# Two-layer hybrid decoder: second layer's parameters and phase tables moved into the first block's last steps, last mixer's score maxima placed later

## The chip, the cores and the metric

One core of one Trainium2 chip. The time is device microseconds of the one core. Before the change three runs took 1578.61, 1579.19 and 1581.76 us; the median is 1579.19 us.

## The reference, cut to what matters

x is 256 tokens by 1024 channels, float32, and there are two layers. Each layer does

```
h = h + concat(deltanet(p), s5(p), diff_attention(p)) @ w_out     with p = rms_norm(h) @ w_in
h = h + peer(rms_norm(h))
```

- `s5`: a diagonal complex state space with 16 groups of 64 states. From lambda and the step come a_bar = exp(lambda * step) and the input scale (a_bar - 1) / lambda; a scan over the tokens follows, then C, a skip, a gelu and a gated linear unit. The kernel runs the scan as a real scan of magnitudes between two rotations, so each layer needs tables of cos and sin of the phase for 128 tokens.
- `diff_attention`: 4 heads with two causal softmaxes each; the output is (p0 - lambda p1) V, normalised. lambda is made of exp(sum(lq1*lk1)) - exp(sum(lq2*lk2)) + a constant.
- `peer`: 8 heads per token, top 16 of 128 on two key sets, top 16 of their 256 sums, and for each of these 128 experts per token u_tab[e] . x, gelu, softmax gate, and a weighted sum of v_tab[e]. An expert's u and v rows are 4 KB each, and every token has its own.

Last comes a final rms_norm.

## The kernel before, in words

**Blocks and steps.** The tokens are cut into two tiles of 128, so there are four blocks (layer, tile), numbered i = 0 to 3. The experts of a block are fetched by 128 steps on u_tab and 128 on v_tab. In step r, GpSimd starts one indirect DMA (`u_gather`) that brings the u row of one expert for each of the 128 tokens (512 KB), VectorE takes its dot product with x (`dot`, L1834, 1.22 us), and a second indirect DMA (`v_gather`) brings a v row whose weighted sum TensorE makes (`values`, four rows at a time, on the places 1, 5, 9, ... of a block). This text says "dot 92 of block 0" for step 92 of block 0. There are 512 dots and 512 v gathers in all.

**Rings.** u rows have 7 buffers: the gather for dot q waits for dot q-7. v rows have 11 buffers, freed in fours by `values`; in GpSimd's program the v gather that needs the `values` of place R stands about where the u gather that needs dot R stands. GpSimd issues both kinds in one order, u then v, so one that waits holds back all behind it.

**The mixer of the next block runs beside the dots.** While the dots of block b run, every engine also works on the mixer (norm, input projection, deltanet, s5, attention, output projection, query projection, key scores) of block b+1. This order is written by hand: `mix(i)`, `attention(i)` and `scans(i)` are generators that yield a place, and `Stages.advance(limit)` (L155) runs, after each dot (on TensorE and ScalarE at the same places of their own programs), all that has a place up to the dot's number. Where two parts have the same place, `mix` goes first. `place(i, slot)` and `attend(i, slot)` squeeze the places for i = 1; for i = 2 and 3 they are the numbers in the code. A place only sets the order within an engine's program. Between engines there are semaphores alone, so an engine that waits in a mixer's step also holds back its next dot or its next `values`.

**Top-k.** In places 2 to 22 of each 32 dots VectorE also runs `top` for the next 32 experts, and in the last places of a block `top(4i)` from the new scores.

**Parameters.** SyncE fetches the weights in blocks of 512 KB into a ring of 4 buffers (`wring`, L590), each when TensorE has freed its buffer. `params(1)` (L533) brings the second layer's four: `cols` (317 KB), C (256 KB, into `sa[:, 1024:1536]`), `rows` (486 KB) and `keysT` (512 KB). It is issued once block 1's key scores are done (L580, L581). `keysT` can't be overwritten before those scores.

**Tables.** `tables(i)` (L1356) on VectorE takes the steps, lambda and the sines (two Sin on ScalarE, `tables_sin`) and makes the cos and sin tables `phase_c`, `phase_s` by seven doublings with a scratch A, B in `sa`. Most of its instructions have 8 to 512 columns with a drain between them. It comes in 12 pieces, for the second layer at places 2 to 29 of block 1 (`mix(2)`, L1545 to L1551). Its first piece waits for the parameters (L1360). `outputs(2)` (L1458) folds C into `cz` at place 37.

**Attention of mixer 3** (a "wide" one: second tile, two rounds of two heads each). Each round takes scores on TensorE, `att_max_of` (VectorE reads the scores' maxima from PSUM, L1515), `att_exps` (ScalarE), `att_scales`, `att_second` (ScalarE), `att_diff` (L1531), and the turn of the probabilities on TensorE. Round one's maxima are at place 71 and round two's at 74.6. TensorE's and ScalarE's places are scores 69 and 73.2, exponentials 71.2 and 74.8, turns 75.9 and 78.3. Between them lie the six levels of deltanet's inverse, each a product (71, 74, 77, 80), a copy on ScalarE (71.6, 74.6, ...), an update (72, 75, ...) and on VectorE the mask of a later level (71.6, 74.6, 77.6), which waits for the product two levels before it.

Of the kernel before, what the change touches and what calls it, by code (L numbers as in the profile page):

```python
# [150 lines left out]

SCANS = (33.0, 41.5, 50.0, 58.0)
# [22 lines left out]
def _build(nc, ctx, x, w_blocks, cols_d, rows_d, keys_d, u_tab, v_tab, cst_d, fin_d, out):  # L175
# [148 lines left out]
    params_in = signal("params_in", 64, 0)  # L324
# [120 lines left out]

    def flat3(a):
        return a.rearrange("p a b -> p (a b)")
# [84 lines left out]
    def _(sp):  # L532
        def params(layer):  # L533
            sp.dma_start(cols[:, :], cols_d[layer, :, 0:HELD_COLS]).then_inc(params_in.sem, 16)
            sp.dma_start(sa[:, 1024:1536], cols_d[layer, :, HELD_COLS:HELD_COLS + 512]).then_inc(params_in.sem, 16)
            sp.dma_start(rows[:, :], rows_d[layer, :, 0:HELD_ROWS]).then_inc(params_in.sem, 16)
            sp.dma_start(keysT[:, :, :].rearrange("p h n -> p (h n)"), keys_d[layer, :, :]).then_inc(params_in.sem, 16)
# [40 lines left out]
        for i in range(1, NI):  # L578
            if i == TB:
                sp.wait_ge(*sc_done(1, 2))  # L580
                params(1)  # L581
            for c, (name, half) in enumerate(CHUNKS):
# [8 lines left out]
                if (name, half) == ("out3", 1):  # L591
                    sp.wait_ge(*ao_done(i, 1))
                    sp.dma_start(g2_row, rows_d[i // TB, 0:1, HELD_ROWS:NROWS]).then_inc(g2_in.sem, 16)

# [12 lines left out]
    def _(pe):  # L607
# [383 lines left out]
        def mix(i):  # L991
# [14 lines left out]
            if layer > 0:  # L1006
                pe.wait_ge(*params_in(layer, 64))
# [210 lines left out]
        def head_scores(i, half, banks):  # L1218
            pe.wait_ge(*pq_ready(i, half + 1))
            for j in range(4):  # L1220
                for a in range(2):
                    r = slice(64 * a, 64 * a + 64)
                    ins = mm(banks[a][:, j * P:(j + 1) * P], qpT[r, 4 * half + j, :], keysT[r, 4 * half + j, :])
# [110 lines left out]
    def _(dve):  # L1334
# [21 lines left out]
        def tables(i):  # L1356

            layer = i // 2
            if layer > 0:
                dve.wait_ge(*params_in(layer, 64))  # L1360
# [69 lines left out]
            while n < P:  # L1430
# [3 lines left out]
                A = sa[:, 1536:2048].rearrange("p (m t) -> p m t", m=MT)[:, :, 0:n]  # L1434
                B = sa[:, 2048:2560].rearrange("p (m t) -> p m t", m=MT)[:, :, 0:n]
# [18 lines left out]
            if layer > 0:  # L1454
                yield 37
                outputs(layer)
# [85 lines left out]
        def mix(i):  # L1542
            t, layer = i % 2, i // 2
            rs = rounds(i)
            if t == 0:  # L1545
                yield place(i, 2)
                made = tables(i)
                for k in made:
                    if k > 32:
                        break  # L1550
                    yield place(i, k)  # L1551
# [5 lines left out]
            if t == 0:  # L1557
                yield place(i, 37)
                next(made, None)
# [96 lines left out]
        def attention(i):  # L1656
# [33 lines left out]
            yield attend(i, 71 if wide else 69.8 + 2 * later)  # L1690
            att_max_of(i, rs[0], *round_heads(i, rs[0]))
            yield attend(i, 72.4 if wide else 71.4 + later)
# [4 lines left out]
            yield attend(i, 74 if wide else 72.8 + later)  # L1697
            att_diff(i, rs[0], *round_heads(i, rs[0]))
            if wide:
                yield attend(i, 74.6)  # L1700
                att_max_of(i, rs[1], *round_heads(i, rs[1]))
            if t == 1:
                yield attend(i, 76 if wide else 73.8)
                att_scales(i, rs[1], *round_heads(i, rs[1]))
                yield attend(i, 77.4 if wide else 75.2)
                att_diff(i, rs[1], *round_heads(i, rs[1]))
            yield attend(i, 82 if wide else 80)
            dve.wait_ge(*ao_ss(i, 1))
            V.reciprocal(dss, dss).then_inc(dss_ready.sem, 1)
            yield attend(i, 83.5 if wide else 81.9)  # L1710
# [423 lines left out]
    def _(act):  # L2134
# [20 lines left out]
        def tables_exp(i):  # L2155
            act.wait_ge(*params_in(i // 2, 64))
# [49 lines left out]
        def mix(i):  # L2206
            t, layer = i % 2, i // 2
            rs = rounds(i)
            if t == 0:
                yield place(i, 1)  # L2210
                tables_exp(i)
                yield place(i, 5)
                tables_sin(i)
# [11 lines left out]
            if layer > 0:  # L2225
                act.wait_ge(*params_in(layer, 64))
# [193 lines left out]
        def scans(i):  # L2420
# [248 lines left out]
        for n in range(NP):  # L2669
            if n % 4 == 0:  # L2670
                b = n // 4
                stages = Stages(mix(b + 1), attention(b + 1), *([scans(1)] if b == 0 else [])) if b + 1 < NI else Stages(final_first())
# [159 lines left out]
```

## Time and profile before

| | us |
|---|---|
| median of three runs | 1579.19 |
| the profiled execution, its time | 1580.82 |
| its span (first to last instruction) | 1579.0 |
| VectorE busy | 1104.1 |
| GpSimd busy (issuing gathers) | 993.9 |
| TensorE busy | 970.5 |
| ScalarE busy | 299.6 |

The DMA engines moved 626.51 MB at a mean of 397 GB/s; 536.94 MB of it are gathers. The span and the profiled execution's time differ by 1.8 us, which lie around the span. The steps of the four blocks begin (dot 0) at 131.96, 470.08, 844.98 and 1214.43 us.

### The profile page before, as it was taken

What the parts mean: (1) busy time and instruction counts of PE and PEld (TensorE: products, weight loads), DVE (VectorE), ACT (ScalarE), POOL (GpSimd) and SP (SyncE); (2) the same over time, 40 slices, a digit from 0 to 9 for tenths busy, and PEclk for the clock granted to TensorE, in tenths of its full rate; (3) what the DMA queues carried; (4) which work ended last, traced back from release to release, by engine and by line L of the source; (5) the groups of instructions that cost most, each with busy time, mean ns of one, the idle gap of its engine ahead of it and who ended that gap; (6) DMA issues with size and microseconds to landing.
All of it is one profiled execution on the core that took longest, in us unless ns stands there. A gap on an engine that the chain in (4) does not pass through costs nothing.

```text
span 1579.0 us, 17672 instructions
## 1 busy us (share of the span) xinstructions
PE 970.5 (61%) x5842; PEld 546.2 (35%) x5842; DVE 1104.1 (70%) x2869; ACT 299.6 (19%) x837; POOL 993.9 (63%) x1034
## 2 busy tenths in 40 slices
PE   9996567967443279886644347978864333333335
PEld 8885445534300046552420025755340000000001
DVE  6849799884648978786486766888466757575440
ACT  7434221321100042241100032324110010000000
POOL 0006666776566776667567775656767777777773
PEclk9997889977756589998876678989875666666558
DMA  9558999999999999999999999999999999999997
GB/s 368 188 200 302 411 393 419 419 419 420 418 420 419 381 417 420 419 419 414 420 419 420 420 419 419 408 418 348 418 419 420 419 419 419 419 419 419 420 419 307
DMA packets 172467, 626.51 MB, mean 397 GB/s; under 512 B 19284, under 2 KB 19412, under 8 KB 172376
## 3 DMA queue, kind: packets, MB, share of 16 engines
q0 software_dynamic: 147456, 536.94, 84.0%
q1 hardware_dynamic: 24920, 88.45, 14.2%
q8 instruction: 46, 0.75, 0.2%
q14 instruction: 45, 0.37, 0.1%
HBM read 624.26 MB, written 1.05 MB: 396 GB/s over the span
## 4 chain that ended last, share of the span: by engine, by line
DMA 28%; DVE 21%; POOL 21%; PE 16%; issue 9%; DVEq 4%; ACT 1%; POOLq 0%; ACTq 0%
DMA uring<-in_u_tab,small 24%; PE ps L609 16%; DVE uring L1834 10%; POOL uring L2688 7%; POOL vring L2688 7%; POOL gd L2688 2%; DMA vring<-in_v_tab,small 2%; POOL wring L2688 1%; DMA uring<-in_v_tab,small 1%; DMA sa<-in_u_tab,small 1%; POOL sa L2688 1%; DVE small L1749 1%; DVE small L1760 0%; DVE sel L1794 0%; DVE small L1802 0%
## 5 line engine op out<-in xcount | busy, mean ns | idle before, releaser
L1834 DVE CUSTOM_DVE_ANT_0 uring<-uring,ps 128x1024 f32<-128x1024 f32 x462 | 558.2, 1217 | 282.9 <-DMA uring<-in_u_tab,small 262.1
L2688 POOL DMA_INDIRECT uring<-in_u_tab,small x462 | 452.6, 980 | 371.9 <-DVE small L1834 168.4
L609 PE MATMUL ps<-vring,wmat 128*32 128x512 f32 x1748 | 320.1, 853 | 361.9 <-DMA vring<-in_v_tab,small 305.9
L2688 POOL DMA_INDIRECT vring<-in_v_tab,small x437 | 417.6, 956 | 154.6 <-issue 127.5
L609 PEld LDWEIGHTS ps<-vring,wmat 128*32 128x32 f32 x1748 | 58.1, 137 | 551.2 <-DMA vring<-in_v_tab,small 369.5
L609 PE MATMUL ps<-hnT,wring 128*128 128x128 f32 x1184 | 150.5, 285 | 0.7 <-DMA wring<-in_w_blocks 0.7
L609 PEld LDWEIGHTS ps<-hnT,wring 128*128 128x128 f32 x1184 | 141.4, 198 | 25.8 <-issue 21.6
L609 PE MATMUL ps<-wring,hnT 128*128 128x512 f32 (+1 forms) x208 | 88.6, 573 | 15.4 <-DMA wring<-in_w_blocks 11.6
L2678 ACT ACTIVATE small<-small 128x32 f32<-128x32 f32 x16 | 3.7, 230 | 465.7 <-DVEq L1843 465.7
L609 PE MATMUL ps<-gd 128*128 128x128 f32 (+1 forms) x518 | 74.2, 296 | 12.8 <-ACT gd L2138 11.2
L2138 ACT ACTIVATE gd<-ps 128x512 f32<-128x512 f32 (+3 forms) x86 | 48.0, 564 | 176.2 <-PE ps L609 161.9
L609 PEld LDWEIGHTS ps<-gd 128*128 128x128 f32 x518 | 68.2, 204 | 31.2 <-issue 15.4
L1834 DVE CUSTOM_DVE_ANT_0 gd<-gd,ps 128x1024 f32<-128x1024 f32 x40 | 48.8, 1220 | 32.6 <-DMA gd<-in_u_tab,small 31.1
L609 PEld LDWEIGHTS ps<-wring,hnT 128*128 128x128 f32 x208 | 41.1, 208 | 56.3 <-issue 49.9
L609 PE MATMUL ps<-phase_c,wmat 128*32 128x512 f32 x28 | 24.9, 1043 | 42.6 <-DMA vbuf<-in_v_tab,small 42.6
L609 PE MATMUL ps<-kT,wmat 128*32 128x512 f32 x28 | 25.0, 1046 | 41.2 <-DMA vring<-in_v_tab,small 34.0
L609 PE MATMUL ps<-wring,wmat 128*32 128x512 f32 x112 | 23.6, 989 | 39.2 <-DMA wring<-in_v_tab,small 32.2
L2435 ACT ACTIVATE small<-small 128x16 f32<-128x16 f32 x32 | 6.6, 209 | 215.9 <-DVE small L1782 215.8
L609 PE MATMUL ps<-sa,cz 128*32 128x128 f32 x224 | 33.5, 325 | 20.8 <-DVEq L1509 20.8
L2688 POOL DMA_INDIRECT gd<-in_u_tab,small x40 | 38.3, 958 | 12.2 <-issue 9.8
L1834 DVE DVE_READ_ACCUMULATOR2_ANT small<- 128x1 f32 x512 | 42.3, 83 | 0.0
L609 PE MATMUL ps<-cst 128*128 128x512 f32 x70 | 39.8, 656 | 1.7 <-ACTq L2176 1.7
(450 smaller groups left out, 1507.3 us busy)
## 6 DMA issues: line engine op xcount, KB each, us to landing
wring<-in_w_blocks SPq DMA_DIRECT2D x120, 512.0 KB, 7.2
vring<-in_w_blocks SPq DMA_DIRECT2D x32, 512.0 KB, 8.6
uring<-in_u_tab,small POOLq DMA_INDIRECT x462, 12.5
vring<-in_v_tab,small POOLq DMA_INDIRECT x437, 11.3
wring<-in_cols SPq DMA_DIRECT2D x3, 512.0 KB, 6.8
h<-in_x SPq DMA_DIRECT2D x2, 512.0 KB, 9.2
keysT<-in_keys SPq DMA_DIRECT2D x2, 512.0 KB, 13.7
rows<-in_rows SPq DMA_DIRECT2D x2, 486.0 KB, 10.6
```

What stands on the lines that cost most here:

```text
L609: return nc.tensor.matmul(o, a, b, start=start, stop=True, skip_group_check=True)
L1749: V.max_index(si[:, hd, a, 0:8], sv[:, hd, a, 0:8], S[:, hd, a, :])
L1834: V.tensor_tensor_reduce(row_, row_, xp, 1.0, 0.0, ALU.mult, ALU.add, dots[:, j:j + 1]).then_inc(dot_done.sem, 1)
L2138: return S.activation(dst, src, ACT.Copy, scale=scale)
L2435: S.activation(gate[:, hd, :], gate[:, hd, :], ACT.Exp, accum_out=gz[:, hd:hd + 1])
L2678: S.activation(gt, gt, ACT.Tanh, scale=GELU).then_inc(gelu_tanh.sem, 1)
L2688: nc.gpsimd.indirect_dma_start(dst, None, table, bass.IndirectOffsetOnAxis(ap=index, axis=0)).then_inc(done.sem, 16)
```

## The change

1. SyncE: `params(1)` now brings only `cols`, C and `rows`, and is issued in block 0's part of the weight loop, behind the load of the last block of the output projection of mixer 1 (`out3`, first half), after a wait for `mix_ready(1)`. `keysT` is fetched alone where `params(1)` stood, on its own semaphore, for which TensorE waits before the key scores of blocks 2 and 3.
2. VectorE and ScalarE: `tables(2)` leaves `mix(2)` and becomes a part of its own beside mixer 1. Its first piece is at place 92 of block 0, the next at 95, 96 and 97, the doublings at 99 to 105 and 106.5. ScalarE's exponential of the steps is at 91.5 and its sines at 92.5. The scratch is in `gd` instead of `sa`. `outputs(2)` stays at place 37 of block 1.
3. VectorE's attention places: in mixer 3 the first maxima go from 71 to 73, scales 72.4 to 75, difference 74 to 76; second maxima 74.6 to 77.6, scales 76 to 79, difference 77.4 to 81; the two steps of the output's norm 82 to 84 and 83.5 to 85.5. In mixer 2 the maxima go from 71.8 to 71.9 and the scales from 72.4 to 72.6. In mixer 1 the maxima go from 69.8 to 70.9 and the scales from 71.4 to 72.1 (before squeezing).

```diff
+TABLES = 92.0
-    params_in = signal("params_in", 64, 0)
+    params_in = signal("params_in", 48, 0)
+    tables_at = [(sa[:, 1536:2048], sa[:, 2048:2560]), (gd[:, 2048:2560], gd[:, 2560:3072])]
...
             sp.dma_start(rows[:, :], rows_d[layer, :, 0:HELD_ROWS]).then_inc(params_in.sem, 16)
-            sp.dma_start(keysT[:, :, :].rearrange("p h n -> p (h n)"), keys_d[layer, :, :]).then_inc(params_in.sem, 16)
...
             if i == TB:
                 sp.wait_ge(*sc_done(1, 2))
-                params(1)
+                sp.dma_start(keysT[:, :, :].rearrange("p h n -> p (h n)"), keys_d[1, :, :]).then_inc(keys_in.sem, 16)
...
+                if i == 1 and (name, half) == ("out3", 0):
+                    sp.wait_ge(*mix_ready(i, 1))
+                    params(1)
...
         def head_scores(i, half, banks):
             pe.wait_ge(*pq_ready(i, half + 1))
+            if i >= TB:
+                pe.wait_ge(keys_in.sem, 32)
...
-            if layer > 0:
-                yield 37
-                outputs(layer)
+        def next_tables(i):
+            yield TABLES
+            for k in tables(i):
+                yield TABLES + 0.5 * k
...
-            yield attend(i, 71 if wide else 69.8 + 2 * later)
+            yield attend(i, 73 if wide else 70.9 + later)
             att_max_of(i, rs[0], *round_heads(i, rs[0]))
-            yield attend(i, 72.4 if wide else 71.4 + later)
+            yield attend(i, 75 if wide else 72.1 + later / 2)
             att_scales(i, rs[0], *round_heads(i, rs[0]))
...
-                yield attend(i, 74.6)
+                yield attend(i, 77.6)
                 att_max_of(i, rs[1], *round_heads(i, rs[1]))
...
-                stages = Stages(mix(b + 1), attention(b + 1), *([scans(1)] if b == 0 else [])) if b + 1 < NI else Stages(final_first())
+                stages = Stages(mix(b + 1), attention(b + 1), *([scans(1), next_tables(TB)] if b == 0 else [])) if b + 1 < NI else Stages(final_first())
+        def next_tables(i):
+            yield TABLES - 0.5
+            tables_exp(i)
+            yield TABLES + 0.5
+            tables_sin(i)
```

## Rows read from the trace of the kernel before

**Rows 1.** The page: gigabytes per second in 40 slices, and the chain by line.

```profile
GB/s 368 188 200 302 411 393 419 419 419 420 418 420 419 381 417 420 419 419 414 420 419 420 420 419 419 408 418 348 418 419 420 419 419 419 419 419 419 420 419 307
...
DMA uring<-in_u_tab,small 24%; PE ps L609 16%; DVE uring L1834 10%; POOL uring L2688 7%; POOL vring L2688 7%; POOL gd L2688 2%; DMA vring<-in_v_tab,small 2%; POOL wring L2688 1%; DMA uring<-in_v_tab,small 1%; DMA sa<-in_u_tab,small 1%; POOL sa L2688 1%; DVE small L1749 1%; DVE small L1760 0%; DVE sel L1794 0%; DVE small L1802 0%
```

**Rows 2.** Busy time by stretches of 20 us; last columns: TensorE clock, DMA share, GB/s.

```profile
520.00:540.00 20.00, 6.87 (x32) 1.19 (x32) 18.17 (x60) 0.00 (x0) 14.78 (x15) 0.59 0.97 367
540.00:560.00 20.00, 4.60 (x24) 0.95 (x28) 18.80 (x40) 1.25 (x3) 14.74 (x16) 0.50 1.01 396
...
1060.00:1080.00 20.00, 17.53 (x98) 10.80 (x99) 16.22 (x46) 8.51 (x25) 11.18 (x12) 0.91 0.93 344
1080.00:1100.00 20.00, 16.84 (x124) 10.97 (x123) 18.03 (x39) 8.79 (x31) 14.56 (x15) 0.91 0.96 353
```

**Rows 3.** Stretches in blocks 0 and 1: PE, PEld, DVE, ACT, POOL busy, clock, DMA share, GB/s.

```profile
372.00:408.00 36.00, 26.62 (x193) 19.59 (x192) 14.54 (x24) 5.61 (x9) 19.50 (x22) 0.81 1.03 419
...
474.00:552.00 78.00, 25.92 (x124) 4.21 (x116) 70.38 (x254) 3.58 (x9) 54.43 (x56) 0.59 1.01 400
```

**Rows 4.** VectorE in the 12 stretches of the table pieces: first piece, and their sum.

```profile
474.51:477.66 3.15, 2.31 (x20) 0.93 1.03 421
...
sum 28.54, DVE 23.09; mean DVE 1.92
```

**Rows 5.** What VectorE waited for, 340 to 408 us.

```profile
DVE uring L1834 <- DMA uring<-in_u_tab,small: 35.9, 20, 3.8
```

**Rows 6.** Timeline: SyncE's load of output blocks 2 and 3, TensorE's use of blocks 0 and 1.

```profile
355.32 0.81 SPq L590 DMA_DIRECT2D wring<-in_w_blocks  x2
...
361.33 8.80 PE L609 MATMUL ps<-wring,hnT 128*128 128x512 f32 x16 [4.18 <-DMA wring<-in_w_blocks]
```

**Rows 7.** DMA issues between 410 and 420 us: size, us from issue to landing.

```profile
rows<-in_rows SPq DMA_DIRECT2D x1, 486.0 KB, 10.9
cols<-in_cols SPq DMA_DIRECT2D x1, 317.0 KB, 6.4
sa<-in_cols SPq DMA_DIRECT2D x1, 256.0 KB, 8.9
```

**Rows 8.** Timeline, GpSimd: u gathers for dots 100 and 112 of block 0.

```profile
361.72 0.94 POOL L2688 DMA_INDIRECT uring<-in_u_tab,small  x1 [0.31 <-issue]
...
397.69 0.94 POOL L2688 DMA_INDIRECT uring<-in_u_tab,small  x1 [1.25 <-DVE small L1834]
```

**Rows 9.** Timeline, VectorE: dots 92 and 112 of block 0.

```profile
352.82 1.22 DVE L1834 CUSTOM_DVE_ANT_0 uring<-uring,ps 128x1024 f32<-128x1024 f32 x1 [1.29 <-DMA uring<-in_u_tab,small]
...
418.40 1.21 DVE L1834 CUSTOM_DVE_ANT_0 uring<-uring,ps 128x1024 f32<-128x1024 f32 x1
```

**Rows 10.** Gather and dot of step 89 of block 1, then of step 94 of block 2.

```profile
714.90 0.94 POOL L2688 DMA_INDIRECT uring<-in_u_tab,small  x1 [0.30 <-issue]
...
723.34 1.22 DVE L1834 CUSTOM_DVE_ANT_0 uring<-uring,ps 128x1024 f32<-128x1024 f32 x1 [0.20 <-DMA uring<-in_u_tab,small]
...
1105.02 0.93 POOL L2688 DMA_INDIRECT uring<-in_u_tab,small  x1 [0.30 <-DVE small L1834]
...
1111.09 1.22 DVE L1834 CUSTOM_DVE_ANT_0 uring<-uring,ps 128x1024 f32<-128x1024 f32 x1 [1.32 <-DMA uring<-in_u_tab,small]
```

**Rows 11.** What VectorE waited for, 1050 to 1093 us.

```profile
DVE small L1515 <- PE ps L609: 5.0, 2, 3.2
DVE small L1709 <- ACT small L2414: 0.9, 1, 0.9
DVE sa L1531 <- ACTq L2183: 0.8, 1, 0.8
```

**Rows 12.** Timeline: exponentials on ScalarE, values of place 73 on TensorE, the next v gather.

```profile
1059.09 0.47 ACT L2174 ACTIVATE sa<-ps,small 128x256 f32<-128x256 f32 x1 [5.03 <-DVEq L1518]
...
1065.30 1.96 PE L609 MATMUL ps<-vring,wmat 128*32 128x512 f32 x16
...
1067.57 0.97 POOL L2688 DMA_INDIRECT vring<-in_v_tab,small  x1 [3.26 <-PE ps L609]
```

More of the change, by code:

```diff
@@ L1006, in mix @@
             if layer > 0:
-                pe.wait_ge(*params_in(layer, 64))
+                pe.wait_ge(*params_in(layer, 48))
             for k in range(KT):
@@ L1359, in tables @@
             if layer > 0:
-                dve.wait_ge(*params_in(layer, 64))
+                dve.wait_ge(*params_in(layer, 48))
                 lam_sums()
@@ L1433, in tables @@
                 nc_, ns_ = pw[1] if n in (1, 4, 16, 64) else pw[0]
-                A = sa[:, 1536:2048].rearrange("p (m t) -> p m t", m=MT)[:, :, 0:n]
-                B = sa[:, 2048:2560].rearrange("p (m t) -> p m t", m=MT)[:, :, 0:n]
+                A = tables_at[layer][0].rearrange("p (m t) -> p m t", m=MT)[:, :, 0:n]
+                B = tables_at[layer][1].rearrange("p (m t) -> p m t", m=MT)[:, :, 0:n]
                 pcb, psb = bc(pc[:, :, None], [P, MT, n]), bc(psn[:, :, None], [P, MT, n])
@@ L1544, in mix @@
             rs = rounds(i)
[L1545 to L1551, printed above, removed]
             if i >= TB:
@@ L1558, in mix @@
                 yield place(i, 37)
-                next(made, None)
+                outputs(layer)
             yield place(i, 42)
@@ L1696, in attention @@
                 att_max_of(i, rs[1], *round_heads(i, rs[1]))
-            yield attend(i, 74 if wide else 72.8 + later)
+            yield attend(i, 76 if wide else 72.8 + later)
             att_diff(i, rs[0], *round_heads(i, rs[0]))
             if wide:
-                yield attend(i, 74.6)
+                yield attend(i, 77.6)
                 att_max_of(i, rs[1], *round_heads(i, rs[1]))
             if t == 1:
-                yield attend(i, 76 if wide else 73.8)
+                yield attend(i, 79 if wide else 73.8)
                 att_scales(i, rs[1], *round_heads(i, rs[1]))
-                yield attend(i, 77.4 if wide else 75.2)
+                yield attend(i, 81 if wide else 75.2)
                 att_diff(i, rs[1], *round_heads(i, rs[1]))
-            yield attend(i, 82 if wide else 80)
+            yield attend(i, 84 if wide else 80)
             dve.wait_ge(*ao_ss(i, 1))
             V.reciprocal(dss, dss).then_inc(dss_ready.sem, 1)
-            yield attend(i, 83.5 if wide else 81.9)
+            yield attend(i, 85.5 if wide else 81.9)
             dve.wait_ge(*ao_scaled(i, 1))
@@ L2155, in tables_exp @@
         def tables_exp(i):
-            act.wait_ge(*params_in(i // 2, 64))
+            act.wait_ge(*params_in(i // 2, 48))
             S.activation(stp, col("lst"), ACT.Exp).then_inc(step_ready.sem, 1)
@@ L2208, in mix @@
             rs = rounds(i)
[L2209 to L2213, printed above, removed]
             yield place(i, 33.5)
@@ L2225, in mix @@
             if layer > 0:
-                act.wait_ge(*params_in(layer, 64))
+                act.wait_ge(*params_in(layer, 48))
             for b, o in enumerate((M0, M1)):
@@ L2671, in _ @@
                 b = n // 4
-                stages = Stages(mix(b + 1), attention(b + 1), *([scans(1)] if b == 0 else [])) if b + 1 < NI else Stages(final_first())
+                stages = Stages(mix(b + 1), attention(b + 1), *([scans(1), next_tables(TB)] if b == 0 else [])) if b + 1 < NI else Stages(final_first())
             for j in range(PAIR):
```

## The prediction

> **What bounds the kernel now.** I read the page's slices first. From slice 7 on the DMA engines move 418 to 420 GB/s nearly everywhere, and the chain of waits names the u gathers first, then VectorE's dots and GpSimd's issue of gathers [rows 1]. A 512 KB gather at 419 GB/s is 1.25 us, so one dot's pair is 2.5 us. The total of bytes is fixed and the change doesn't alter it. So the time falls only by what it removes of the idle time of the DMA engines, and rises by what it adds. Then I read the stretches of 20 us, to price the dips. 520 to 560 us lacks (419-367)/419*20 + (419-396)/419*20 = 3.6 us; 1060 to 1100 us lacks 3.6 + 3.15 = 6.7 us [rows 2]. The first dip is that of the tables: from 474 to 552 us VectorE is busy 70.4 of 78 us, the rest being drains, and the DMA engines move 400 GB/s, which is again 3.6 us short [rows 3]. The second lies in mixer 3's attention, where VectorE waits 5.0 + 0.9 + 0.8 = 6.7 us for others [rows 11].
>
> **The tables leave block 1.** Twelve pieces take 28.5 us of VectorE [rows 4]. Without them VectorE needs far less than the 80 us that the DMA engines need for these 32 dots, so the dip's 3.6 us come back. They cannot bring more: outside the dip there was no idle time to recover. Bounds 3 to 4 us. Gain 3.6.
>
> **The tables enter block 0.** In the old trace the place looks made for them: from 340 to 408 us VectorE waits 35.9 us for gathers [rows 5]. But the first piece waits for the parameters, on the engine that runs the dots.
> - Issue. SyncE loads output blocks 2 and 3 at 355.3 and is done at 356.1 [rows 6]; `mix_ready` is given by then. The three parameter DMAs follow up to 357.4.
> - Landing. Alone in SyncE's queue they landed 6.4, 8.9 and 10.9 us after their issue [rows 7]; that would be 368.2. Here four weight loads stand in front. TensorE gets the first two at 361.33 [rows 6]. Rows 7 show `rows` (486 KB) landing about 2.5 us behind C, which is half of 419 GB/s; at that rate two more loads end at 366.3 and the 1059 KB behind them (1.5 + 1.2 + 2.4) at 371.4. I take 371.4, since the first pair's wait is a row of this very place.
> - VectorE ends dot 92 at 354.0 [rows 9] and then stands until 371.4. Queued behind the wait are dots 93 and on; for dot 93 waits the u gather 100, and behind that every later gather on GpSimd. With the first piece (3.15 us) VectorE is free at 374.6, dot 93 ends at 375.7, and gather 100 is issued 14 us later than its 361.72 [rows 8]. ScalarE stands too, but has nothing due.
> - After that VectorE is full: up to dot 106 it has 13 dots (14.8 us), 23 us of pieces (28.5 less the first and, by estimate, 2.2 for the last), and by estimate 4 us of gelu, residual and norm (14.5 busy in 372 to 408 less ten dots, and the part before 372 [rows 3]). That is 3.2 us per dot against 2.5: it doesn't catch up here.
> - What the DMA engines notice. At 397.7 the old kernel issues gather 112 [rows 8]; the new one is at gather 106. It lacks 6 pairs (15.0 us) and four query weight loads (5.0 us), which wait for TensorE, hence for the norm of dot 98; it has 2.6 us of parameters more. Shortage 17.4 us. The spare: gather 112 took at most 20.7 us to its dot [rows 8, 9], while in block 1 a gather took 8.4 us and in block 2 one took 6.1 us with the engines still nearly full [rows 10]. So 12.3 to 14.6 us of the queue could be lost free of charge, and 2.8 to 5.1 us of idle time remain. I take 4.0, their middle. With the landing at 368.2 it would be about 0.8; with VectorE 4 us later still, 8. So 1 to 8.
>
> The Trainium skill, DMA: Bandwidth & Descriptors, section on queues, rings and completion order, says that each DMA engine alternates between the queues it has work for, packet by packet. By it the parameters get half of the bandwidth but stay behind SyncE's own four loads, which is the 371.4 and the 4.0; by the landing times of rows 7 alone it would be the 368.2 and the 0.8. The half rate in rows 7 agrees with the rule.
>
> **keysT alone, and its wait on TensorE.** It is issued where it was, most of a block ahead of its use (block 1 starts at 470 us, block 2 at 845): nothing, covered by block 1's mixer. `outputs(2)` stays. The scratch in `gd` costs what that in `sa` does.
>
> **Attention of mixers 1 and 2.** For mixer 2, 71.8 to 71.9 and 72.4 to 72.6 cross no dot and no other step: nothing. For mixer 1 maxima and scales move one dot; the DMA engines are full there, and they can only change the spare by about 1 us either way. Taken as 0.
>
> **Attention of mixer 3.** Placed two dots later, the first maxima no longer wait for TensorE's scores. But VectorE arrives, by its dots and top-k steps, at about 1058.3, after the scores are there; so the maxima end some 0.8 us later than before, not earlier. ScalarE's exponentials hang on them (it waited 5.0 us for them at 1059.09), behind these the copy for level 3, TensorE's update, the `values` of place 73 at 1065.30, and the v gather that GpSimd holds back until 1067.57 [rows 12]. That v gather, not the dot, is the last wait in this place; it gets later by 0.8. The second maxima, at place 77.6, stand behind the mask of level 6 and come out at about 1076.5 against 1073; TensorE's turn and the `values` of place 77 follow some 2.6 us later, and so does the v gather on them. VectorE meanwhile runs some 5 us ahead and then waits for the output's norm. By my walk through the four programs GpSimd is even with the old kernel again at about 1091. So 0. Bounds: all 6.7 us back if TensorE's chain keeps its time, 2 us lost if the chain's delay lasts.
>
> **Sum.** The profiled execution took 1580.8: -3.6 + 4.0 + 0 gives 1581.2. It stands 1.6 us above the median of the runs, so for a median 1579.6 us. A measurement tells about 0.2%, 3.2 us, from no change; this is within it.
>
> **Rivals.**
> 1. *The old idle time is real room* (faster). The parameters land near 368, or the queue's spare is as large as 20 us; then block 0 costs 0 to 1 instead of 4, and in mixer 3 VectorE's freed waits reach GpSimd for about half of 6.7. Time: 1579.2 - 3.6 + 0.5 - 3.3 = 1572.8. For it: 35.9 us of waits against 28.5 us of tables, and that VectorE's waits and the DMA engines' loss in mixer 3 are the same 6.7 us. Against it: the order of waits worked out above.
> 2. *The parameter wait becomes the bound* (slower). Place: VectorE behind dot 92, about 354 to 371 us, and the dots up to 108 that follow without a gap. Price: each microsecond of VectorE's lag above about 12 us is a microsecond of idle DMA; with the landing at 374 or ScalarE's sines late, the lag is 18 to 20 and the price 8, with the mixer's chain 1 more. Time: 1579.2 - 3.6 + 9 = 1584.6. For it: the latencies of rows 8 to 10 leave no more than 15 us. Against it: the dots of this place were waiting anyway.
> 3. *The change does not do what it says*: the tables' dip goes, block 0 gives the same back, and the attention's places only exchange one wait for another. That is the forecast itself.
>
> **How the numbers follow.** Forecast (within 0.2%) 0.42; rival 1, 0.33; rival 2, 0.25. The forecast's own range is 1576 to 1583. To hold 8 in 10 the range takes in most of rival 1 and rival 2: 1571 to 1585. Faster 0.33, same 0.42, slower 0.25.
>
> **What would show it.** Stretches of 20 us from 500 to 560 at 419 GB/s; if not, the first gain is wrong. A VectorE wait of 15 to 18 us at the first table instruction in block 0 and a dip of some 4 us between 385 and 430: absent, rival 1; twice as deep, rival 2. In mixer 3 no wait of L1515 for TensorE, a later wait at L1709 of some 4 us, and a GpSimd wait for TensorE of 6 to 7 us at place 73; a dip of 5 to 8 us in 1060 to 1100 as before. If that dip shrinks to 3 us, my reading of who holds back GpSimd is wrong.

## The result, and the profile after

The changed kernel took 1585.82 us, median of 7 runs (1583.68 to 1589.93), the kernel before 1581.07 us beside it (7 runs, 1578.61 to 1583.1). The ratio is 1.0040, 95% interval 1.0029 to 1.0050: 6.3 us slower by the ratio, 4.75 by the two medians. The profiled execution of after took 1585.07 us (span 1583.3) against the 1580.82 of before, so 4.25 us are to be found between the two traces. The forecast was 1579.6 us and "within 0.2%", with a range up to 1585.0: the median lies 0.8 us above its top, and a real loss stands where none was forecast. In some of the sets of runs below, each with its own runs of the kernel before on the same chip, every kernel took 1690 to 1745 us (one run of the move alone 2110) and scattered by 2%, so that a ratio from them tells little under 0.4%; they are called scattering sets.

First the page of after: gigabytes per second in 40 slices.

```profile
GB/s 371 183 200 307 406 404 419 419 419 392 396 420 420 419 419 420 419 404 410 420 419 420 420 419 419 419 415 324 419 419 420 419 419 419 419 419 420 419 419 299
```

Counted from slice 0, and against [rows 1], the dip of slice 13 (381) has gone, two new ones stand in slices 9 and 10 (392, 396), one in slices 17 and 18 (404, 410), and the old one of slice 27 is deeper (324 for 348). Now the same by stretches of 20 us; last columns TensorE's clock, DMA share, GB/s.

```profile
380.00:400.00 20.00, 9.17 (x44) 4.59 (x48) 17.10 (x76) 3.92 (x6) 10.51 (x12) 0.50 0.93 350
400.00:420.00 20.00, 19.08 (x172) 14.70 (x164) 18.10 (x63) 1.68 (x3) 11.83 (x13) 0.99 1.00 390
...
520.00:540.00 20.00, 7.28 (x32) 1.19 (x32) 11.26 (x23) 0.00 (x0) 15.12 (x17) 0.50 1.02 419
540.00:560.00 20.00, 7.79 (x35) 1.79 (x36) 12.76 (x28) 4.11 (x6) 15.12 (x17) 0.50 1.03 420
...
680.00:700.00 20.00, 15.82 (x90) 10.19 (x94) 18.31 (x49) 7.70 (x26) 9.07 (x10) 0.83 1.01 405
700.00:720.00 20.00, 15.44 (x120) 10.01 (x112) 14.57 (x30) 11.05 (x37) 15.42 (x16) 1.00 1.00 391
...
1060.00:1080.00 20.00, 14.63 (x70) 9.15 (x70) 15.99 (x37) 6.35 (x19) 7.51 (x9) 0.83 0.83 308
1080.00:1100.00 20.00, 16.07 (x124) 10.31 (x124) 14.92 (x35) 10.78 (x30) 13.30 (x14) 1.00 0.93 337
```

Each stretch is turned into idle time of the DMA engines as in the prediction, (419 - GB/s)/419*20. For before, 380 to 420 moved 419 in both stretches and 680 to 740 moved 419, 414 and 414.

| idle DMA, us | 380 to 420 | 500 to 560 | 680 to 740 | 1060 to 1100 |
|---|---|---|---|---|
| before | 0 | 3.8 | 0.5 | 6.7 |
| after | 4.7 | 0 | 2.2 | 9.2 |
| difference | +4.7 | -3.8 | +1.7 | +2.5 |

The differences sum to 5.1; a dip of 1.0 us at 980 to 1000, which before has and after has not, brings that to 4.1, and the two executions differ by 4.25. Both moved the same bytes, so the idle time of the whole span has to differ by just that; the rest (0.8 us less ahead of 380, 0.8 more behind the last gathers) cancels. The new dip in block 0 is nearly paid for by the old one in block 1, and what is left over lies in the attentions of mixers 2 and 3.

How much of such a difference one execution can carry is seen where the programs are the same. Eight of the eleven profiles outside the scattering sets ("undisturbed" below) are of kernels with the same work up to 340 us; their idle time ahead of 380 us is 59.0 to 62.7. At 680 to 740, before and the three kernels that differ from it only in mixer 3 have 0.5, 1.0, 2.1 and 0.4. So the +1.7 there isn't clear of the scatter; the +4.7 and -3.8 are. At 1060 to 1100 the six with both old rounds of mixer 3 have 4.1 to 6.7, the three with both new ones 7.6 to 9.2.

Block 0, timeline of after: SyncE's parameter issues, VectorE's first table instruction, GpSimd's u gather for dot 100.

```profile
353.91 0.43 SPq L537 DMA_DIRECT2D cols<-in_cols  x1
354.38 0.44 SPq L538 DMA_DIRECT2D sa<-in_cols  x1
354.86 0.43 SPq L539 DMA_DIRECT2D rows<-in_rows  x1
...
370.31 0.23 DVE L1352 CUSTOM_DVE_ANT_0 small<-rows 128x64 f32<-128x64 f32 x1 [17.91 <-DMA rows<-in_rows]
...
374.94 0.94 POOL L2690 DMA_INDIRECT uring<-in_u_tab,small  x1 [13.13 <-DVE small L1835]
```

The parameters landed by 370.3 (371.4 forecast) although they were issued some 2 us earlier than forecast, VectorE stood 17.9 us (17.4), and the gather went out at 374.94 (375.7 forecast). The Trainium skill, DMA: Bandwidth & Descriptors, section on queues, rings and completion order, has each engine take packets from its queues in turn; by it the parameters, behind SyncE's own loads, were to be late in this way. The 15.4 us from the issue of `rows` to VectorE's start, against 10.9 in [rows 7], agree.

Mixer 3's attention in block 2, timeline of after: the first maxima on VectorE, the exponentials on ScalarE, the update and `values` on TensorE, the v gather on GpSimd.

```profile
1057.30 1.22 DVE L1835 CUSTOM_DVE_ANT_0 uring<-uring,ps 128x1024 f32<-128x1024 f32 x1 [2.78 <-DMA uring<-in_u_tab,small]
...
1059.68 1.27 DVE L1523 TENSOR_REDUCE small<-ps 128x2 f32<-128x512 f32 x2
...
1061.26 0.47 ACT L2175 ACTIVATE sa<-ps,small 128x256 f32<-128x256 f32 x1 [8.74 <-DVEq L1526]
...
1063.94 3.78 PE L614 MATMUL ps<-gd 128*128 128x128 f32 x16 [6.08 <-ACT gd L2139]
1067.66 2.69 PE L614 MATMUL ps<-vring,wmat 128*32 128x512 f32 x16
...
1070.66 0.94 POOL L2690 DMA_INDIRECT vring<-in_v_tab,small  x1 [10.36 <-PE ps L614]
```

Set against [rows 12]: exponentials 2.2 us later, `values` of place 73 2.4 us later and 0.7 longer, the v gather 3.1 us later. GpSimd, which waited 3.26 us for TensorE, waits 10.36. Some 0.6 us of this is no work of the attention: block 2 itself begins 0.55 us later (845.53 for 844.98), and counted from its first dot the v gather is 2.5 us later (225.1 for 222.6). The maxima now stand behind dot 73, and dot 73 itself had to wait 2.78 us for its gather. TensorE's granted clock, 0.91 of full speed at 1060 to 1080 before, is 0.83 after.

### The profile page after: what moved, and what is told of

Read it like the earlier page. It is cut to its first block, busy times and chain, and to the rows that moved or that the text cites. A ratio compares the mean times of both kernels' runs of the same rounds, so it can differ in the third digit from the quotient of the medians.

```text
span 1583.3 us, 17676 instructions
## 1 busy us (share of the span) xinstructions
PE 968.7 (61%) x5842; PEld 545.1 (34%) x5842; DVE 1105.9 (70%) x2869; ACT 299.8 (19%) x837; POOL 992.0 (63%) x1034
## 4 chain that ended last, share of the span: by engine, by line
DMA 30%; POOL 21%; DVE 19%; PE 16%; issue 9%; DVEq 3%; ACT 1%; ACTq 0%; SPq 0%; POOLq 0%
DMA uring<-in_u_tab,small 21%; PE ps L614 16%; DVE uring L1835 9%; POOL vring L2690 8%; POOL uring L2690 8%; DMA vring<-in_v_tab,small 4%; DMA gd<-in_u_tab,small 3%; POOL gd L2690 2%; DMA rows<-in_rows 1%; DMA uring<-in_v_tab,small 1%; POOL wring L2690 1%; DVE small L1761 0%; DVE sel L1795 0%; DVE small L1803 0%; PE ps L617 0%
## 5 line engine op out<-in xcount | busy, mean ns | idle before, releaser
L614 PE MATMUL ps<-gd 128*128 128x128 f32 (+1 forms) x518 | 74.6, 297 | 16.6 <-ACT gd L2139 15.1
## 6 DMA issues: line engine op xcount, KB each, us to landing
uring<-in_u_tab,small POOLq DMA_INDIRECT x462, 12.6
```

The lines of the kernel that those rows point to most:

```text
L614: return nc.tensor.matmul(o, a, b, start=start, stop=True, skip_group_check=True)
```

## The experiments

All times are against the kernel before, run beside it on the same chip, and the difference in us is (ratio - 1)*1580. What fell on a scattering set was measured again (ending in _b, _c). No kernel but the one before was measured on two undisturbed sets, so how far a ratio itself moves from set to set isn't known. The ledger of idle DMA is worked out as above, from one profiled execution each.

Theories at the outset. **T1**: the loss is made in mixer 3's attention, and the move of the tables is about neutral. **T2**: VectorE's wait for the parameters is what it costs. **T3**: the one place in mixer 2 does.

### The move alone, and the places alone

`move_only` is the changed kernel with this undone; `places_only` is the kernel before with this done:

```
-            yield attend(i, 71 if wide else 69.8 + 2 * later)
+            yield attend(i, 73 if wide else 70.9 + later)
-            yield attend(i, 72.4 if wide else 71.4 + later)
+            yield attend(i, 75 if wide else 72.1 + later / 2)
...
-            yield attend(i, 83.5 if wide else 81.9)
+            yield attend(i, 85.5 if wide else 81.9)
```

> The changed kernel with every attention place of before: only the parameters and the tables move. T1 (the loss is made in mixer 3's attention, by the first maxima that come later and the chain ScalarE's exponentials, TensorE's update, `values`, v gather behind them; the move gives 3.7 us back in block 1 and costs 4.0 to 4.7 in block 0): 0 to +1.5 us against before, so 1579 to 1581 us, with the dip at 380 to 420 us and none at 520 to 560, and a v gather of place 73 that waits 3 us for TensorE as before. T2 (VectorE's 17.9 us for the parameters behind dot 92 are what the change costs, by a lag carried on): +4 to +6 us, as the whole change.

> The kernel before with the attention places of the change, nothing else. T1: +3.5 to +5.5 us (2.6 us of idle DMA in 1060 to 1100, 1.6 in mixer 2's attention at 680 to 720, and what follows from them). T2: within 1 us of before.

In a scattering set: 1.0040 (0.9997 to 1.0083) and 1.0043 (1.0003 to 1.0083), which decides nothing. Again:

> The changed kernel with every attention place of before, a second measurement for the same reason. T1: 0 to +1.5 us against before (4.0 to 4.7 us lost at 380 to 420 us, 3.7 gained at 500 to 560). T2: +4 to +6 us.

> The kernel before with the attention places of all mixers from the change, nothing else; a second measurement, since the first stood on runs that scatter by 2%. T1 (the loss is made in the attention places): +3.5 to +5.5 us against before, with the v gather of place 73 in block 2 some 3 us later after the block's start. T2 (the parameter wait of block 0 costs it): within 1 us of before.

The move alone: 1.0019 (1.0010 to 1.0027), +3.0 us. The places alone: 1.0030 (1.0021 to 1.0039), +4.7 us. T1 is right of the size of all places together and wrong of the move, which isn't neutral; T2 is too large for the move and wrong of the places. T1's sign was smaller than expected: the v gather of place 73 was to come some 3 us later after the block's start and came 1.3 later (223.9 us for 222.6). The stretches of 20 us of the move alone:

```profile
380.00:400.00 20.00, 8.32 (x43) 4.41 (x46) 17.07 (x76) 3.92 (x6) 10.53 (x12) 0.60 0.91 341
400.00:420.00 20.00, 18.80 (x172) 14.72 (x164) 17.92 (x63) 1.69 (x3) 11.83 (x13) 1.00 1.00 388
...
680.00:700.00 20.00, 15.79 (x96) 10.85 (x98) 17.08 (x49) 7.95 (x27) 9.91 (x12) 0.91 1.02 410
700.00:720.00 20.00, 15.71 (x120) 10.08 (x112) 15.98 (x32) 10.83 (x37) 15.42 (x16) 1.00 1.01 398
720.00:740.00 20.00, 13.92 (x56) 4.74 (x56) 12.79 (x27) 1.34 (x5) 15.12 (x17) 0.83 1.02 408
```

5.2 us idle in block 0, none at 520 to 560, and 2.0 us at 680 to 740, where before had 0.5, with every attention place of before. That third stretch was in no theory; by the scatter given above it proves nothing by itself.

### Which mixer's places

`mixer3_places` takes over only the `wide` numbers, `mixers12_places` only the others:

```
-            yield attend(i, 71 if wide else 69.8 + 2 * later)
+            yield attend(i, 71 if wide else 70.9 + later)
-            yield attend(i, 72.4 if wide else 71.4 + later)
+            yield attend(i, 72.4 if wide else 72.1 + later / 2)
```

> The kernel before with the new places of mixer 3's attention alone (maxima and scales two to four places later; mixers 1 and 2 as before). T1: +2.5 to +4 us, the v gather of place 73 issued about 3 us later after the start of block 2 than before. T2: within 1 us of before. T3 (it is the one place in mixer 2, by VectorE's and TensorE's order there): within 1 us of before.

> The kernel before with the new places of mixers 1 and 2 alone (first maxima 69.8 to 70.9 and scales 71.4 to 72.1 in mixer 1, 71.8 to 71.9 and 72.4 to 72.6 in mixer 2). T1: 0 to +1.6 us, the 1.6 us that stretches 680 to 720 lack. T3: +3 us or more. T2: within 1 us of before.

First measured beside the two above, in the same scattering set: 1.0021 (0.9978 to 1.0065) and 1.0024 (0.9985 to 1.0062). Again:

> The kernel before with the new places of mixer 3's attention alone, a second measurement, since the first stood on runs that scatter by 2%. All places together measured a ratio of 1.003 (+3.9 to +4.7 us). T1: mixer 3 makes most of it, +2.5 to +4 us, in 1060 to 1100 us. T3 (mixer 2's attention makes it, 680 to 740 us): within 1 us of before.

> The kernel before with the new places of mixers 1 and 2 alone, a second measurement for the same reason. T1: 0 to +1.6 us. T3: +3 us or more, by 680 to 740 us or by mixer 1's attention near 320 us.

Mixer 3: 1.0009 (1.0000 to 1.0018), +1.4 us. Mixers 1 and 2: 0.9997 (0.9987 to 1.0008), -0.5 us, so T3 falls. Mixer 3 costs something, less than T1 expected. But the two together are +0.9 us, give or take 2.1, where the places of all mixers gave +4.7, give or take 1.4. That doesn't add up, and it stays open.

### The two rounds of mixer 3

```
-            yield attend(i, 71 if wide else 69.8 + 2 * later)
+            yield attend(i, 73 if wide else 69.8 + 2 * later)
```

and the scales to 74.2, the difference to 74.4 (`mixer3_first`); or only

```
-                yield attend(i, 74.6)
+                yield attend(i, 77.6)
```

with the four places behind it, as in the change (`mixer3_second`).

> The kernel before with only mixer 3's first round later (maxima 71 to 73, scales 72.4 to 74.2, difference 74 to 74.4; the second round's maxima stay at 74.6). T1 (first maxima, exponentials, copy, update, values of place 73): GpSimd's v gather there waits 8 to 10 us for TensorE instead of 3.1 to 3.3, and the stretches 1060 to 1100 lack 8 to 9 us of full DMA instead of the 5.2 to 6.7 of the kernels with the old places; +1.5 to +2.5 us. Rival T5 (the second round's maxima at 77.6 are what costs, by `values` of place 77): wait of 3 us at place 73 and within 1 us of before.

> The kernel before with only mixer 3's second round later (maxima 74.6 to 77.6, scales 76 to 79, difference 77.4 to 81, the output's norm 82 to 84 and 83.5 to 85.5). T1: GpSimd waits 3 us at place 73 as before; within 1 us of before. T5: +1.5 to +3 us, a second wait of GpSimd for TensorE of 3 us or more near 1080 us.

First round: 1.0029 (1.0017 to 1.0041), +4.6 us. Second round: 1.0029 (1.0018 to 1.0040), +4.6 us. GpSimd's long waits for TensorE near places 73 and 77 of block 2, first round and then second round:

```profile
1066.95 1.02 POOL L2688 DMA_INDIRECT vring<-in_v_tab,small  x1 [6.59 <-PE ps L609]
```

```profile
1066.05 0.94 POOL L2688 DMA_INDIRECT vring<-in_v_tab,small  x1 [3.25 <-PE ps L609]
...
1083.96 0.94 POOL L2688 DMA_INDIRECT vring<-in_v_tab,small  x1 [8.29 <-PE ps L609]
```

Of the second round the place is shown: GpSimd waits 8.29 us for the `values` of place 77, where before has no such wait, and 1060 to 1100 lacks 11.5 us for 6.7. Of the first round it is not. GpSimd's wait at place 73 is longer (6.59 us for 3.26), but it comes to it earlier: the v gather itself goes out 222.7 us after the block's first dot, against 222.6 in before, and 1060 to 1100 lacks 6.6 us, as before. The expectation (a wait of 8 to 10 us, 8 to 9 us of idle time, +1.5 to +2.5 us) missed in all three. The profile is of the fastest of six runs (1581.29, their median 1583.69), so where the first round's 4.6 us lie is open. The second chain can be read off step by step, on VectorE, TensorE and TensorE:

```profile
1075.38 1.28 DVE L1515 TENSOR_REDUCE small<-ps 128x2 f32<-128x512 f32 x2
...
1078.98 1.11 PE L612 MATMUL ps<-cst,sa 128*128 128x128 f32 x4 [4.33 <-ACTq L2176]
1080.02 3.64 PE L609 MATMUL ps<-vring,wmat 128*32 128x512 f32 x16
```

TensorE stands 4.33 us for the exponentials, and the `values` behind the wait take 3.64 us, where [rows 12] have 1.96: nearly double, and TensorE's granted clock over just these matmuls is the lower of its two levels (0.50 of 2.4 GHz; the rows are in the last section). The stretch 1080 to 1100 of this run moved 252 GB/s, 8.0 us idle; before has 3.2. So T1's denial of the second round was wrong, and T5, which put all of the cost there, is right of that place, with more time than its +1.5 to +3, and wrong in denying the first round a cost. Where both are later, GpSimd's second wait is 3.04 us, not 8.29 (the changed kernel, and the places alone): the first wait has by then put everything back, and the second maxima hide behind it. That is a reason for the pair not to be worth 9 us, but not for its +1.4 being less than the first round's +4.6 by itself; that stays open. What mixer 3's places cost together is measured as +1.4 alone (at most 2.8); all places cost +4.7 on the kernel before and, as the difference of two ratios (+6.3 less +3.0), +3.3 on top of the move, give or take 2.1. In the seven profiles with the old first round the v gather of place 73 came 219.6 to 222.9 us after the first dot of block 2, in the four with the new one 222.7 to 225.1. I take 2 to 4 us, an estimate; no run narrows it.

### The wait for the parameters

The tables six dots later, with the attention places of before:

```
-TABLES = 92.0
+TABLES = 98.0
```

> The changed kernel with every attention place of before, and the tables begun at dot 98 of block 0 instead of dot 92 (the parameters are issued where the change issues them, 15.4 us before they land). T1b (what the move costs is VectorE's wait for the parameters behind dot 92, 5.2 us of idle DMA at 380 to 420 us in the run of the move alone): that idle time goes down to 0 to 1.5 us, block 1's 3.7 us stay gained, so -2 to -4 us against before, and 4.5 to 6.5 below the move alone. Rival T4 (the tables' own 28.5 us of VectorE are what block 0 can't carry, and the wait only comes first): the idle time comes 15 us later in the same size, 0 to +3 us against before.

0.9992 (0.9983 to 1.0000), -1.3 us; against the move alone (1.0019) 4.3 us less, give or take 1.9, from two sets. The wait behind dot 92 was what the move cost, by T2's mechanism and less than T2's size: 380 to 420 us moved 420 and 419 GB/s. But not all idle time of block 0 went; it fell from 5.2 to 2.5 us:

```profile
440.00:460.00 20.00, 7.29 (x32) 1.19 (x32) 18.27 (x39) 0.51 (x4) 12.16 (x12) 0.50 0.97 367
...
443.93 1.86 POOL L2690 DMA_INDIRECT uring<-in_u_tab,small  x1 [4.30 <-DVE small L1835]
```

2.5 us are idle where the pieces meet the top-k steps of the block's last rows; T4 is true to that extent. A second measurement of it:

> Tables begun at dot 98, attention places of before, a second measurement. If the parameter wait is what the move costs and block 1's gain is given back: within 1.5 us of before (first ratio 0.9992), and 3 us or more below the move alone (1.0019 of before).

0.9996 (0.9957 to 1.0034), in a scattering set: in line, and no more. Then the pieces spread:

```
-                yield TABLES + 0.5 * k
+                yield TABLES + 0.8 * k
```

> As the kernel with the tables begun at dot 98 (attention places of before), but its pieces 0.8 of a dot apart instead of 0.5, so that the last and largest of them come at places 117 to 121, behind the top-k steps of the block's last rows. The run at dot 98 still lost 2.5 us at 440 to 460 us, where VectorE did table pieces and top-k steps between two dots and GpSimd waited 4.3 us for it. If that is the cause, the dip goes to under 0.7 us: -2.5 to -4 us against before, and the fastest kernel of this study. T4 (block 0 can't carry the tables' 28.5 us at all): a dip of 2 to 3 us comes elsewhere in 400 to 480, within 1.5 us of before.

The dip went as expected (440 to 460 moved 419), and so all idle time in blocks 0 and 1 that the tables had made, in either place. The time did not follow: 1.0005 (0.9996 to 1.0014), +0.8 us. This expectation fell outright, and its stretches show new idle time behind it:

```profile
440.00:460.00 20.00, 7.00 (x36) 1.19 (x32) 18.31 (x51) 0.00 (x0) 13.18 (x14) 0.67 1.03 419
...
520.00:540.00 20.00, 7.29 (x36) 1.19 (x32) 10.83 (x23) 0.00 (x0) 15.13 (x17) 0.67 1.03 419
...
680.00:700.00 20.00, 15.55 (x98) 10.31 (x98) 18.57 (x52) 8.47 (x28) 10.08 (x11) 0.91 0.92 354
700.00:720.00 20.00, 12.55 (x98) 8.41 (x102) 15.79 (x31) 10.29 (x36) 15.28 (x16) 0.91 1.02 404
```

680 to 740 now lacks 4.2 us, where before lacked 0.5 and no kernel of the same places with the tables in block 1 more than 2.1.

### Leaving the tables out

From this a new theory, **G**: what is won ahead of mixer 2's attention is given back in it. It is tried in the kernel before, by leaving out the seven doubling pieces of the second layer's tables (its second layer works on the first one's tables, so its later experts, and with them the rows gathered, need not be those of before); nothing is moved:

```
-            while n < P:
+            while n < (P if layer == 0 else 1):
```

> The kernel before, with the seven doubling pieces of the second layer's tables (about 20 of the 28.5 us of VectorE in block 1) left out, so its second layer works on the first one's tables; parameters, places and all else as before. Theory G (given back: mixer 2's attention, paced by TensorE's chain scores, update, `values`, is reached earlier and the DMA engines stand longer there): the dip at 500 to 560 us goes from 3.6 us to under 0.5, stretches 680 to 740 lack 2 to 4 us instead of 0.5, the v gather behind place 73 of block 1 comes 222 to 223 us after the block's start as before, and the time falls by 0 to 1.5 us. The forecast's own theory (idle DMA time removed is time gained): -3 to -4 us, 680 to 740 as before.

> The kernel before with the seven doubling pieces of the second layer's tables left out; a third measurement, since two scattered by 2%. Theory G (given back in mixer 2's attention, paced by TensorE): no dip at 500 to 560 us, 2 to 4 us of idle DMA at 680 to 740 instead of 0.5, the v gather behind place 73 of block 1 some 222 to 223 us after the block's start, 0 to 1.5 us faster. The forecast's own theory (idle DMA time removed is time gained): 3 to 4 us faster.

Taken three times, since the first two fell on scattering sets: 0.9983 (0.9947 to 1.0019), 0.9991 (0.9953 to 1.0029) and then, among runs of 1577 to 1583 us, 1.0002 (0.9993 to 1.0012). So +0.3 us, at best -1.1, for a kernel whose VectorE is busy 12.6 us less (1091.5 for 1104.1; the expectation's 20 us was an estimate with the drains): the 3 to 4 us are ruled out. Its stretches:

```profile
520.00:540.00 20.00, 7.08 (x40) 1.22 (x36) 11.94 (x25) 0.00 (x0) 15.12 (x17) 0.67 1.03 414
540.00:560.00 20.00, 8.41 (x53) 2.05 (x45) 14.10 (x37) 6.39 (x14) 15.12 (x17) 0.70 1.03 420
...
680.00:700.00 20.00, 15.28 (x99) 10.12 (x98) 18.40 (x56) 8.89 (x28) 10.03 (x11) 0.91 0.93 355
700.00:720.00 20.00, 12.84 (x101) 8.26 (x104) 15.95 (x27) 9.87 (x35) 15.43 (x16) 0.90 1.02 409
720.00:740.00 20.00, 14.93 (x61) 5.49 (x54) 9.47 (x20) 1.08 (x2) 15.12 (x17) 0.93 1.02 406
```

The dip of 3.8 us is down to 0.7, and 680 to 740 lacks 4.2 for 0.5: 3.1 won, 3.7 given back. The rest of this one execution's ledger differs too (2.7 us less ahead of 380, where the programs are the same, and 2.2 less at 1060 to 1100), and it was 2.1 us shorter than the profiled one of before; the price is the ratio's, the place is the profile's. Here is the place, on VectorE, TensorE and GpSimd:

```profile
679.52 1.29 DVE L1515 TENSOR_REDUCE small<-ps 128x4 f32<-128x512 f32 x2 [0.94 <-PE ps L609]
...
684.78 3.44 PE L609 MATMUL ps<-gd 128*128 128x128 f32 x16 [3.35 <-ACT gd L2138]
688.14 2.12 PE L609 MATMUL ps<-vring,wmat 128*32 128x512 f32 x16
...
690.58 0.94 POOL L2688 DMA_INDIRECT vring<-in_v_tab,small  x1 [6.93 <-PE ps L609]
```

And the same in before, where the maxima didn't wait:

```profile
686.76 3.57 PE L609 MATMUL ps<-gd 128*128 128x128 f32 x16 [3.35 <-ACT gd L2138]
...
692.49 0.94 POOL L2688 DMA_INDIRECT vring<-in_v_tab,small  x1 [6.51 <-PE ps L609]
```

So the waits of TensorE and GpSimd are those of before, to 0.4 us. What differs is how much is queued at the DMA engines while GpSimd stands. Up to 220 us (2.4 us before that v gather) after the first dot of block 1 each kernel has issued the same 388 gathers since the start, 203.4 MB; the gather queue had moved this much of them (packets, MB, share), in before and with the doubling left out:

```profile
q0 software_dynamic: 55065, 200.54, 72.2%
```

```profile
q0 software_dynamic: 55462, 201.98, 72.5%
```

That leaves 2.9 MB in the queue in before, 6.9 us of work at 419 GB/s, and 1.4 MB, 3.4 us, here. The dip that was taken out is a shorter queue, and the same stand of GpSimd empties it. All eleven undisturbed profiles agree: with the tables in block 1 (six) 6.9 to 7.9 us were queued at this moment and 680 to 740 lacked 0.2 to 2.1; without them (five, the changed kernel among these) 2.8 to 4.9 us were queued and 2.0 to 4.2 were lacking.

VectorE's own lead is gone before that. From the first dot of block 1 to dot 36 of it, before took 93.7 us, this kernel 88.9 and the changed one 88.1; to dot 56, 158.7, 160.2 and 158.6, though no DMA engine stood idle in between in any of them. And the v gather of place 73 goes out 222.4 us after the block's first dot in before, 222.6 here and 222.5 in the changed kernel: it keeps its time, whatever was won ahead of it. Over the eleven profiles it came after 222.4 to 224.0 us where block 1 had its tables (six) and after 221.8 to 222.6 where it had not (five), so about 1 us of the 3.8 gets through. That TensorE's chain is what holds the mixer's end in place is read from these waits; it wasn't tried by shortening that chain.

### The whole change again

> The changed kernel unaltered. If its loss is the move's (+3.0 by ratio) and the places' (+4.7): +5 to +8 us; the first pair of profiles had +4.2. A v gather of place 73 in block 2 that waits 8 to 10 us for TensorE, 4 to 5.5 us of idle DMA at 380 to 420 us.

1.0045 (1.0015 to 1.0075), +7.1 us, and in one more measurement (six runs) 1.0151 (1.0094 to 1.0208), both in scattering sets, where the profile no longer has the features asked for (GpSimd's longest waits for TensorE near there were 11.3 and 7.5 us, at other times). They confirm the side. Whether the whole is exactly the sum of the parts (+3.0 and +4.7 against +6.3) they can't tell.

No version beat the kernel before by what can be told. The best is the one with the tables begun at dot 98, 1.3 us faster with an interval that ends at 1.0000.

## Why the prediction was wrong

The forecast is 6.2 us below the median. Of these, 1.9 lie in its base: it started from three runs of before (1579.19), and the seven beside the changed kernel had 1581.07. The other 4.3 are the change, +4.75 by the medians for the forecast's +0.4.

- **What bounds the kernel**: right as a description, wrong as a rule for the sum. "So the time falls only by what it removes of the idle time of the DMA engines" took idle time as if it could be taken out of one stretch without a word from the next. GpSimd's stands are tied to dots and to TensorE's chain, so idle time taken out ahead of one only means that the queue is shorter when it comes.
- **"Gain 3.6" for the tables leaving block 1**: the first step that failed. It was taken as time won in full. The dip went as forecast (419, 419 and 420 GB/s at 500 to 560). The time did not: leaving the doubling out gains nothing (1.0002), and its idle time comes back as 3.7 us in mixer 2's attention. In the changed kernel itself, where block 0's new dip comes first, 1.7 us more are idle there, within the scatter. "They cannot bring more: outside the dip there was no idle time to recover" set a bound above, and the bound of 3 below had no reason given. In before, 680 to 740 was nearly full only because the dip had come first and left more in the queue.
- **"I take 4.0" for block 0**: right. 4.7 us in after and 5.2 in the move alone, by the steps given: landing 370.3 for 371.4, wait 17.9 for 17.4, gather at 374.9 for 375.7. Taking the wait away (tables at dot 98) gave 4.3 us of time back, give or take 1.9.
- **keysT, scratch**: right in so far as no profile shows a wait at either; not tried alone.
- **Attention of mixers 1 and 2, 0**: -0.5 us, interval -2.1 to +1.3. The term stands, with the reserve that the parts of the places don't add.
- **"So 0" for mixer 3**: the second step that failed. The chain was named in the right order, and mis-sized. The first maxima were put 0.8 us later, and came 2.2 later (1059.68 for 1057.50), since dot 73, now ahead of them, waited 2.78 us for its gather; the v gather went out 3.1 us later for the 0.8 forecast, GpSimd waited 10.4 us at place 73 for the 6 to 7 that were named as the sign, and 1060 to 1100 lacked 9.2 for the 5 to 8. (In the three other kernels with the new first round dot 73 waited 0.2 to 1.0 us, and the v gather came 0.1 to 1.5 us later than in before, from the block's start.) The second round was put at 2.6 us and then written off as made up by 1091; measured alone it costs 4.6 us of time (interval 2.8 to 6.3). "2 us lost if the chain's delay lasts" as a bound was too near. What was said of VectorE is right: it no longer waits at the maxima in after, and waits 3.7 us later for the output's norm.
- **The rivals**: rival 2 named the slower side with a time of 1584.6, near the 1585.8 measured, by a mechanism that did happen and was no larger than in the forecast itself (4.7 us for the 4.0, and not 8): that its time fits is luck. Rival 1 is refuted in both parts: block 0 cost 4.7 us of idle time and not 0 to 1, and mixer 3 gave nothing back. Rival 3, taken as the forecast, described blocks 0 and 1 well and left out what comes after them.
- **The sum as it should have been**: +4.7 in block 0, about -1.7 in block 1 (move alone +3.0 by time, so that this is the remainder, between -3.1 and -0.4; leaving the doubling out says at best -1.1), and +2 to +4 for mixer 3. That makes 5 to 7, and 6.3 was measured; since the remainder and the range for mixer 3 come from the same ratios, this is an account and not a second proof.

## What to carry to other kernels

Idle time of the bottleneck is not yet gain: before it goes into a sum as won, find the next place where the engine that issues the transfers stands still for another engine, and set what is queued during that stand against how long it is (here 6.9 us queued for 6.5 of standing, and 3.4 for 6.9). The cheapest test is to leave the suspected work out, and look both at its own stretch and at the next two. And a step that is put behind one more dot inherits the wait of that dot (0.2 to 2.8 us here in four kernels): price it by the time its gather can land, and not by VectorE's own speed alone.

## What was not expected of the hardware

- **Whole runs at 8% less speed.** In three sets the kernel before took 1704.63, 1712.26 and 1707.06 us for the 1579 to 1581 of the others. The page of the move alone in such a set, DMA busy in tenths and GB/s:

```profile
DMA  9459999799999999989999999999999989999996
GB/s 373 162 194 338 397 417 378 273 369 341 388 417 391 370 363 369 416 319 351 416 419 419 373 362 402 409 415 357 409 401 369 416 344 368 389 379 350 355 362 255
```

  The ceiling of 419 GB/s is the same, and reached only in some slices; in most others the DMA engines are marked busy at 340 to 400. What takes the bandwidth isn't in the trace, and nothing was tried on it. Two things in the record narrow it. It isn't a fixed trait of one chip: the chip that the record numbers 6 gave the first of these sets, and about an hour later one with the kernel before at 1579.14. And in all nine profiles of the three sets the same slices are hit: slices 19 and 20 moved 416 to 420 in each, slice 32 339 to 353 and slice 33 365 to 371, where the undisturbed profiles have 419 or 420. The Trainium skill, HBM Reference, section Specifications (TRN2), says that the two cores of a domain share its bandwidth, about 358 GB/s each when both stream; a busy neighbour would fit the size of the low slices, but no run here shows one, and it would have had to keep step with this kernel nine times. An edit of this size can't be judged in such a set: the whole change gave 1.0045 and 1.0151 there, for 1.0040.
- **TensorE's clock was low behind its waits.** The 16 matmuls of `values` took 1.96 us in before, 2.69 in after and 3.64 in the run with the second round later, each soon after TensorE had waited (2.4, 6.1 and 4.3 us). Over just these matmuls, in this order (third column from the end: granted clock, as a share of 2.4 GHz; 0.50 is the lower level, 1.2 GHz):

```profile
1065.30:1067.26 1.96, 1.96 (x18) 0.50 (x17) 1.08 (x4) 1.39 (x3) 0.00 (x0) 0.97 1.03 405
```

```profile
1067.66:1070.35 2.69, 2.69 (x18) 0.59 (x17) 1.88 (x7) 1.39 (x3) 0.00 (x0) 0.70 0.47 187
```

```profile
1080.02:1083.66 3.64, 3.64 (x18) 0.66 (x17) 3.31 (x6) 1.57 (x4) 0.00 (x0) 0.50 0.08 32
```

  So 0.7 us of the v gather's delay in after, and 1.7 us in the run with the second round later, go with the clock and not with the steps of the chain. That the wait is what brought the clock down is the likely reading; nothing was tried on it.
